# Work moved from VectorE to GpSimd in the attention part of a one-core decoder step

## The reference, cut to what matters

```python
h = rms_norm(x, norm_attn)                       # then one input projection of h
o_sb  = stick_breaking(sb_q, sb_k, sb_v)         # 8 heads x 64, causal
p2    = softmax(q k_sel); o_sel = p2 @ v_sel     # 8 heads, 2 kv groups
pw    = softmax(q k_win); o_win = pw @ v_win
o_nsa = g0 * o_cmp + g1 * o_sel + g2 * o_win     # per-head sigmoid gates
mix   = concat(rms_norm(o_sb, norm_sb_out), rms_norm(o_nsa, norm_nsa_out))
x     = x + mix @ w_out
h2    = rms_norm(x, norm_ffn)                    # rows for the router and the experts
y     = top-1 of 4 groups, top-2 of 4 gated experts on h2
out   = rms_norm(x + y, norm_final)
```

## Time and profile before

| what | value |
|---|---|
| median of three runs | 818.14 us |
| lowest, highest | 817.3, 818.15 us |
| profiled execution: span | 814.9 us |
| between the span and the median run | 3.2 us |
| PE busy | 736.1 us (90%) |
| DVE busy | 381.6 us (47%) |
| ACT busy | 218.5 us (27%) |
| POOL busy | 56.9 us (7%) |

### The profile page before, as it was taken

The page is one execution under the profiler, slowest core; times in us unless marked ns, Lnnn a source line. Parts: engine busy times, 40 slices in busy tenths (PEclk is TensorE's granted clock), DMA queues, the critical chain, the costliest instruction groups (busy, mean ns, idle before and its releaser), DMA issues.

```text
span 814.9 us, 12490 instructions
## 1 busy us (share of the span) xinstructions
PE 736.1 (90%) x4713; PEld 397.4 (49%) x4713; DVE 381.6 (47%) x884; ACT 218.5 (27%) x561; POOL 56.9 (7%) x87
## 2 busy tenths in 40 slices
PE   4986899997999788989979977789999999999987
PEld 2454456444645544545545643355555545454532
DVE  5421103385220667886877845365144332423145
ACT  1211111111221446656756831001110101010113
POOL 0111000120000000000000000210000000000040
PEclk9999899999999579999999998689999999999999
DMA  9136881558334960000000246789899999999992
GB/s 329 33 92 168 236 308 44 199 140 271 115 132 123 288 252 1 1 3 1 1 27 1 104 153 235 223 265 335 284 400 407 402 406 396 408 402 399 408 389 108
DMA packets 99423, 172.98 MB, mean 212 GB/s; under 512 B 21314, under 2 KB 38562, under 8 KB 99330
## 3 DMA queue, kind: packets, MB, share of 16 engines
q1 hardware_dynamic: 87986, 150.76, 52.3%
q10 hardware_dynamic: 8112, 11.24, 3.7%
q0 software_dynamic: 3264, 10.17, 3.5%
HBM read 152.95 MB, written 21.28 MB: 214 GB/s over the span
## 4 chain that ended last, share of the span: by engine, by line
PE 56%; DVE 8%; DMA 5%; ACT 4%; issue 3%; SPq 1%; ACTq 0%; DVEq 0%
PE bank L2392 18%; PE bank L1797 5%; PE bank L2825 5%; PE bank L2383 4%; PE bank L2807 4%; PE bank L2426 4%; PE bank L1724 3%; PE bank L1743 3%; DMA reg<-w_down 2%; PE bank L2516 1%; PE bank L2511 1%; SPq L1965 1%; DMA work<-h_rows,ids 1%; PE bank L1726 1%; PE bank L2375 1%
## 5 line engine op out<-in xcount | busy, mean ns | idle before, releaser
L2825 PE MATMUL bank<-reg 128*128 128x512 f32 (+1 forms) x384 | 165.8, 578 | 1.2 <-DVE reg L2766 0.9
L2392 PE MATMUL bank<-reg,qreg 128*32 128x128 f32 (+2 forms) x848 | 130.4, 389 | 0.8 <-issue 0.8
L2825 PEld LDWEIGHTS bank<-reg 128*128 128x128 f32 x384 | 71.7, 195 | 69.4 <-issue 66.7
L2392 PEld LDWEIGHTS bank<-reg,qreg 128*32 128x32 f32 (+2 forms) x848 | 66.8, 139 | 59.5 <-issue 48.2
L2807 PE MATMUL bank<-cf,reg 128*128 128x128 f32 (+1 forms) x384 | 63.2, 285 | 24.0 <-DVE reg L2757 9.9
L1797 PE MATMUL bank<-reg 128*128 128x512 f32 x128 | 65.9, 640 | 0.4 <-DVE x L1504 0.3
L2807 PEld LDWEIGHTS bank<-cf,reg 128*128 128x128 f32 (+1 forms) x384 | 43.3, 145 | 42.1 <-issue 35.4
L2682 ACT ACTIVATE work<-bank 128x128 f32<-128x128 f32 (+6 forms) x107 | 40.9, 413 | 45.3 <-PE bank L2807 44.7
L2766 DVE COPY work<-bank 128x128 f32<-128x128 f32 (+4 forms) x56 | 23.2, 429 | 51.0 <-PE bank L2807 50.8
L1212 ACT ACTIVATE reg<-bank,st 128x128 f32<-128x128 f32 (+3 forms) x64 | 33.2, 525 | 35.5 <-DVE st L1372 35.4
L1743 PE MATMUL bank<-work,vreg 128*64 128x128 f32 x480 | 39.2, 295 | 2.4 <-DVE work L2766 2.4
(11 more groups left out here) (338 smaller groups left out, 929.4 us busy)
## 6 DMA issues: line engine op xcount, KB each, us to landing
reg<-w_gate SPq DMA_DIRECT2D x12, 2048.0 KB, 20.2
reg<-w_up SPq DMA_DIRECT2D x12, 2048.0 KB, 23.9
reg<-w_down SPq DMA_DIRECT2D x12, 2048.0 KB, 20.8
reg<-w_in SPq DMA_DIRECT2D x16, 512.0 KB, 5.9
expert_rows<-vreg SPq DMA_DIRECT2D x11, 512.0 KB, 5.3
reg<-cache_sb_k SPq DMA_DIRECT2D x16, 256.0 KB, 4.4
reg<-cache_sb_v SPq DMA_DIRECT2D x16, 256.0 KB, 4.6
qreg<-w_up SPq DMA_DIRECT2D x2, 2048.0 KB, 16.6
```

The lines of the kernel that those rows point to most:

```text
L2392: ins = T.matmul(bank[which][rows, at_:at_ + w], rowsT[b][:, k, r0:r0 + n], w_[:, k, h * w:(h + 1) * w], start=(k == 0), stop=(k == KD - 1))
L2825: ins = nc.tensor.matmul(at("m", ("proj", n))[:, 0:w], hT[:, k, i * P:(i + 1) * P], win[:, pos % 2, k, 0:w], start=(k == 0), stop=(k == KD ...
```

## The change

- `share`: DVE only inverts the sums. POOL scales the probabilities, with the inverse and the gate as two per-row factors in one instruction a head (64 instructions of 128 x 128 to 128 x 512).
- `scale_wout`: POOL does it, in eight steps of one block, from agenda place 15 on, every 40 units.
- `mix_sums`: POOL does it, for all five tiles, as two additions of two inputs (512 and then 256 elements a row) in place of one reduction.
- `h2` of the decode tile, tile 0 and tile 1 (`POOL_ROWS`): POOL does it, as a scaling by the row's factor and a product with the gain (1024 elements a row each) in place of one DVE instruction. Tiles 2 and 3 stay on DVE.
- `top`: one maximum instruction over both heads' banks in place of two.
- Some semaphores are merged, and the router's weights get one of their own.

The diff, cut to its core:

```diff
+    POOL_ROWS = tile_order[:3]
...
-    for q, k in enumerate(range(0, KD, 2)):
-        place((60, 130, 230, 330)[q], scale_wout, k)
+    for k in range(KD):
+        place(15 + 40 * k, scale_wout, k)
...
+    def unit_sums(u):
+
+        q = nsa_at[u] % 4
+        return st[:, 2 * q:2 * q + 2]
...
     def gps_more(pool, kind, key):
-        if kind == "slots":
+        G = nc.gpsimd
+        if kind == "share":
+            i, b, p = key
+            n, w = (i + 1) * P, unit_sums(key)
+            gate = gate_rows(i)[:, b, p, :]
+            if key == nsa_units[0]:
+                sg.wait(pool, "gates", 0)
+            sg.wait(pool, "inverse", key)
+            for e in range(2):
+                prob = prob_of(key, e)[:, 0:n]
+                ins = G.tensor_scalar(prob, prob, w[:, e:e + 1], gate[:, e:e + 1], ALU.mult, ALU.mult)
+            ins.then_inc(sg["shared"], 1)
+        elif kind == "scale_wout":
+            k0, = key
+            if k0 == 0:
+                pool.wait_ge(sg["gain_in"], 64)
+            pool.wait_ge(sg["w_out_sb" if k0 < REP else "w_out_nsa"], 16 if k0 < REP else 32)
+            G.tensor_scalar(w_out[:, k0, :], w_out[:, k0, :], gainT[:, k0:k0 + 1], None, ALU.mult
+                            ).then_inc(sg["w_scaled"], 1)
+        elif kind == "mix_sums":
+            i, = key
+            r = ROWS[i]
+            four = squares[:, :, 0:r].rearrange("p (b k) q -> p b k q", b=2)
+            sg.wait(pool, "squares", i)
+            if i != QT:
+                sg.wait(pool, "t_full", ("ssq", tile_order[tile_order.index(i) - 1]))
+            G.tensor_tensor(four[:, :, 0:2], four[:, :, 0:2], four[:, :, 2:4], ALU.add).then_inc(sg["square_sums"], 1)
+            sg.wait(pool, "square_sums", ("half", i))
+            G.tensor_tensor(square_sums[:, :, 0:r], four[:, :, 0], four[:, :, 1], ALU.add).then_inc(sg["square_sums"], 1)
+        elif kind == "h2" and key[0] in POOL_ROWS:
+            i, = key
+            r = ROWS[i]
+            sg.wait(pool, "rstd", ("ffn", i))
+            G.tensor_scalar(h2[0:r], x[0:r, i, :], small[0:r, 12:13], None, ALU.mult).then_inc(sg["h2"], 1)
+            sg.wait(pool, "h2", ("normed", i))
+            G.tensor_tensor(h2[0:r], h2[0:r], gain[0:r, :], ALU.mult).then_inc(sg["h2"], 1)
+        elif kind == "slots":
...
-            for e, ring in enumerate(("ga", "gb")):
-                top = 32 + 2 * (q % 4) + e
-                sg.wait(dve, ring + "_full", key)
-                V.tensor_reduce(st[:, top:top + 1], at(ring, key)[:, 0:n], AX.X, ALU.max, negate=True
-                                ).then_inc(sg["arg"], 1)
+            top = 32 + 2 * (q % 4)
+            sg.wait(dve, "ga_full", key)
+            sg.wait(dve, "gb_full", key)
+            V.tensor_reduce(st[:, top:top + 2], psum[:, 2:4, 0:n], AX.X, ALU.max, negate=True).then_inc(sg["arg"], 1)
         elif kind == "share":
-            i, b, p = key
-            n, q = (i + 1) * P, nsa_at[key]
-            w = st[:, 2 * (q % 4):2 * (q % 4) + 2]
-            gate = gates[:, i, :].rearrange("p (g r t) -> p r t g", g=GROUPS, r=REP)[:, p, b, :]
+            w = unit_sums(key)
             sg.wait(dve, "gb_act", key)
-            link(V.reciprocal(w, w))
-            link(V.tensor_tensor(w, w, gate, ALU.mult))
-            for e in range(2):
-                ins = V.tensor_scalar(prob_of(key, e)[:, 0:n], prob_of(key, e)[:, 0:n], w[:, e:e + 1], None, ALU.mult)
-            ins.then_inc(sg["shared"], 1)
+            V.reciprocal(w, w).then_inc(sg["inverse"], 1)
```

More of the change, by code:

```diff
@@ L462, in norm @@
             step("norm", i)
-            sg.mark(f"x{i}", i, 16)
+            sg.mark(f"tile{i}", i, 16)
             sg.mark("ssq", ("attn", i))
@@ L597, in mix_sums @@
         step("mix_sums", i)
+        sg.mark("square_sums", ("half", i))
         sg.mark("square_sums", i)
@@ L628, in ffn_scale @@
         sg.mark("rstd", ("ffn", i))
+    POOL_ROWS = tile_order[:3]
     def ffn_rows(i):
         step("h2", i)
+        if i in POOL_ROWS:
+            sg.mark("h2", ("normed", i))
         sg.mark("h2", i)
@@ L701, in top @@
         step("top", *u)
-        sg.mark("arg", u, 2)
+        sg.mark("arg", u)
     def exp(u):
@@ L708, in share @@
         step("share", *u)
+        sg.mark("inverse", u)
         sg.mark("shared", u)
@@ L854, in body @@
     route_weights(QT - 1)
-    for name, by in (("const", 16), ("const_b", 16), ("gain_attn", 16), ("table_zero", 16), ("y_zero", 16 * EXTRA + 16), ("router_in", 80),
-                     ("iota", 1), ("zero", 1), ("act_chain", 0), ("dve_chain", 0), ("pe_chain", 0)):
+    for name, by in (("const", 32), ("gain_attn", 16), ("table_zero", 16), ("y_zero", 16 * EXTRA + 16), ("router_in", 80),
+                     ("iota", 1), ("zero", 1), ("act_chain", 0), ("dve_chain", 0), ("pe_chain", 0),
+                     ("router_scaled", 1)):
         sg.mark(name, 0, by)
@@ L998, in load_router @@
     def load_router(sp):
-        sp.dma_start(cb[:, :], a["const_b"]).then_inc(sg["const_b"], 16)
+        sp.wait_ge(sg["const"], 16)
+        sp.dma_start(cb[:, :], a["const_b"]).then_inc(sg["const"], 16)
         sp.wait_ge(sg["zero"], 1)
@@ L1400, in dve_more @@
                 dve.wait_ge(sg["router_in"], 80)
[L1401 to L1406, removed]
+                V.tensor_tensor(wr[:, :, 0:20], wr[:, :, 0:20], gainR[:, :].unsqueeze(2).to_broadcast([P, KD, 20]), ALU.mult
+                                ).then_inc(sg["router_scaled"], 1)
         elif kind == "sample_small":
@@ L1465, in dve_more @@
                             ).then_inc(sg["c_max"], 1)
[L1466 to L1473, removed]
         elif kind == "cmp_norm":
@@ L1515, in dve_more @@
                                    small[0:r, 12:13]).then_inc(sg["ssq"], 1)
-        elif kind == "h2":
+        elif kind == "h2" and key[0] not in POOL_ROWS:
             i, = key
@@ L1706, in pe_more @@
             if key == units[SEL]:
-                pe.wait_ge(sg["const_b"], 16)
+                pe.wait_ge(sg["const"], 32)
                 for j in range(len(proj)):
@@ L1779, in pe_more @@
                 if i == QT:
-                    sg.wait(pe, "w_scaled", 4 * group + 2)
+                    sg.wait(pe, "w_scaled", 4 * group + 3)
                 if i == QT and group == 0:
@@ L1804, in pe_more @@
             acquire(pe, "t", ("parts", i))
+            if i == QT:
+                pe.wait_ge(sg["router_scaled"], 1)
             for half in range(2):
@@ L2355, in expert_dve @@
             if i == 0:
-                dve.wait_ge(sg["gain_final"], 16)
+                sg.wait(dve, "gain_in", "final")
             sg.wait(dve, "ssq_final", i)
@@ L2620, in _ @@
                     src = a["x_prompt"][0, i * P:(i + 1) * P, :] if i < QT else a["x_sample"][:, 0, :]
-                    sp.dma_start(x[0:ROWS[i], i, :], src).then_inc(sg[f"x{i}"], 16)
+                    sp.dma_start(x[0:ROWS[i], i, :], src).then_inc(sg[f"tile{i}"], 16)
                     if i == 0:
@@ L2746, in _ @@
                 r = ROWS[i]
-                dve.wait_ge(sg[f"x{i}"], 16)
+                dve.wait_ge(sg[f"tile{i}"], 16)
                 if i >= 2:
```

4 lines of the change are left out of this document (2 added, 2 removed).

## The result

The changed kernel takes 828.27 us (median of 4 runs, 826.04 to 830.2) against 818.14; the ratio is 1.013 with a 95% interval of 1.0101 to 1.016. It is slower by some 10 us. I had forecast 820.4, with 817.3 to 823.5 as its own range and 811 to 828 around all the rivals: the sign was right, the size was wrong, and so was the make-up of the sum.

What follows compares the result with a forecast made beforehand. PE was taken to set the end, with its attention stalls for DVE and ACT deciding. 5.7 + 0 - 2.9 - 0.8 - 1.3 + 0.4 + 0.6 (longer half clock) + 0.6 = +2.3, so 820.4 us (817.3 to 823.5; all rivals 811 to 828).

Steps and rivals of the forecast that it cites:

- R3: Rival: POOL scaling with two pointer factors costs 2 to 4 ns an element, normed rows end late; 828 us, chance 0.10.
- Normed rows, decode tile and tile 0, +5.7: Attention: POOL's rows delay ACT's DMA by 2.9 us at tile 0 and 2.8 at the decode tile; bounds +3.5 to +20.
- Tile 1, 0: Normed rows of tile 1: POOL is free early enough, so no cost; range -1.1 to +3 us.
- W_out's rows, -2.9: Opening, 300 to 320 us: moving these rows off DVE shortens PE's waits, by 1.3 and 1.6 us.
- clock -0.8: Opening, 316 to 319.4 us: shorter waits keep PE's clock full, saving 1.6 us at one chance in two.
- opening -1.3: Stretch from 264 to 300 us: PE gains a third of the 4.5 us it lacks.
- step 4: Opening: PE's clock staying full, -0.8 us at one chance in two, and a third of 4.5 us from 264 to 300, -1.3.
- Square sums, +0.4: `mix_sums` on POOL takes 2.1 us against 1.92; only the last tile's makes PE wait longer, 0.1 to 1.2 us.
- Shares on POOL, 0: Shares take 1.4 us a unit against 0.98 on DVE, covered by some 5 us before their transposes; no cost.
- Ports, +0.6: POOL and DVE in each other's way where they overlap: +0.6 us in the sum.
- R4: Rival: DVE and POOL take turns at the ports for whole instructions, delaying DVE's two-input scans; 824 us, chance 0.10.
- One maximum, 0: Scores: one maximum for two saves a fixed cost of about 0.1 us, hidden behind PE's second score; 0.

Runs made afterwards that it cites:

- before_sync: The kernel before with the stores of the first two normed tiles issued by SyncE and nothing else: 812.23 us, ratio 0.9948.
- two_factors_sync: The changed kernel with 1.0 as second factor in POOL's scalings and the first two normed tiles' stores issued by SyncE: 807.24 us, ratio 0.9887.
- experiments 2 and 3: The changed kernel with normed rows back on DVE (809.34 us, 0.9936), then with W_out's rows back on DVE too (808.73 us, 0.9888).
- (7): The changed kernel, one-factor scaling kept, with the stores of the three normed tiles issued by SyncE instead of ACT: 813.48 us, ratio 0.9953.
- experiment 9: The changed kernel with shares, W_out's rows and normed rows on DVE: 0.9985; the kernel before with one maximum for two heads and nothing else: 0.9983.
- rows_by_sync: The changed kernel with only the stores of the three normed tiles moved from ACT to SyncE: 813.48 us, ratio 0.9953.
- rows_dve: The changed kernel with all normed rows back on DVE, W_out's rows staying on POOL with one factor: 809.34 us, ratio 0.9936.
- (10): The changed kernel with 1.0 as second factor and SyncE's stores for two normed tiles: 807.24 us; the kernel before with those stores only: 812.23 us.

## Why the prediction was wrong

The step that failed is the price of a scaling on POOL, 1.2 us for 1024 elements "since one operand is a tensor in both". It was read from the copy and applied to two forms. For the shares, which have two factors, it holds (0.82 against 0.68). For the eleven instructions with one factor it is 2.85 (W_out's rows, mean) and 2.83 to 3.75 (normed rows). R3 had the right fear but for the wrong form: it priced scaling "with two pointer factors" at 2 to 4 ns, and gave 828 us for it, at a chance of 0.10. Mending the form takes 8 of the 10 us away and gives 820.8, my forecast to half a microsecond, but that is partly luck, since other terms were off and cancelled. Term by term:

1. *Normed rows, decode tile and tile 0, +5.7.* By the ruler, these two pairs are 5.0 and 5.8 us longer than before (9.60 to 14.60 and 10.82 to 16.58). Of the excess over 5.7, 3.3 us are the scaling's price (twice 1.65); the other 1.8 go with a lower granted clock behind the longer stalls, 0.79 from 360 to 380 and 0.75 from 420 to 440 (rows below), where the kernel before had 0.92 from 340 to 360 and 0.91 from 400 to 420. The pairs between, 18th to 25th, took 48.05 us in place of 46.10, but that is not shown to be the clock's: in before_sync and two_factors_sync, with shorter stalls, they took 48.03 and 48.04. And the proper base was not the kernel before. Kept on DVE, the rows would have come sooner than before. Seen so, the move costs 16 to 17 us (experiments 2 and 3), of which 14 hang on ACT's queue (7). The changed kernel's stretches behind the two stalls, PE busy and clock as in the windows above:

```profile
360.00:380.00 20.00, 17.20 (x91) 8.88 (x92) 7.90 (x23) 12.35 (x30) 5.29 (x7) 0.79 0.02 3
...
420.00:440.00 20.00, 14.31 (x81) 8.04 (x83) 12.21 (x25) 11.25 (x24) 6.57 (x7) 0.75 0.08 28
```

2. *Tile 1, 0.* The store there goes 14.4 us later than before, and at tile 0 it goes 12.3 us later. Of the 2 us between, 1.4 lie from the 32nd inverse to the store (6.59 to 7.95), in the range, and 0.6 elsewhere.
3. *W_out's rows, -2.9, clock -0.8, opening -1.3.* The 300 to 320 stretch did gain 2.6 us and its clock stayed up, as step 4 had it one time in two. The 264 to 300 stretch lost 4.2 us where I had +1.3, because eight instructions of 2.85 us stand between the shares. "100 units of agenda time or more" was true for W_out's rows themselves, and said nothing about the shares queued behind them. In the sum the opening was worth 0.8 us (ruler 79.3 to 78.5), not 5.0. With 1.1 us each it would have been worth 3.9 to 8.1: the ruler is 71.2 to 75.4 us in the four kernels with that form. (The third of 4.5 us in step 4 is 1.5 and not 1.3, so my own sum would have been +2.1.)
4. *Square sums, +0.4.* PE waits 1.9 us for the last tile's; before it was 1.7. That is the 0.2 by which 2.1 exceeds 1.92, and not 0.4.
5. *Shares on POOL, 0.* They were hidden where they ran, as I said. But what they freed was worth 8 us (experiment 9), at least in front of the normed rows. I had written that between these places less of DVE's load buys nothing, and overlooked that at the normed rows the shares stood in front of the rows in DVE's queue.
6. *Ports, +0.6; R4 at 3 to 4 us.* DVE does stand behind POOL's instructions, as R4 said, and at tile 0 and the decode tile that makes PE stand 6.1 us once ACT is out of the way (7). But not every overlap costs it the whole rest: in the changed kernel one scan of the opening took 1.62 us in place of 0.42 and one at tile 1 took 2.07 in place of 1.20, while the other scans took at most 0.35 more than alone. Two comparisons would size its part together with the longer way of the rows: 0.0017 or 1.4 us with one factor (rows_by_sync over rows_dve, whose store still waits in ACT's queue) and 0.0046 or 3.8 us with two (10). Neither is clear of its intervals, so R4's 3 to 4 us are neither shown nor ruled out; what decided lay elsewhere.
7. *One maximum, 0.* Not told from zero (9).

Together: the shares, sums and maximum -9, W_out's rows about +4 in their form, the normed rows +16 to 17: +11 to 12 by parts, +10.6 measured. The +4 for W_out's rows is the weakest of these, as its intervals overlap. What stays open is how much of the normed rows' cost is the clock and how much the waits, of PE for ACT and for DVE; they came together here. Nor was it tried why the form with one factor is slow.

## What to carry to other kernels

Price an operation on another engine by its exact form, not by its number of tensor inputs: on this chip's GpSimd a scaling by one factor took 2.85 us for 1024 elements and the same with a second factor of 1.0 took 1.1. When a step is moved off an engine, compare with what that engine would then do, not with what it did: the 8 us that one move gained (the shares) were spent, and more, by another (the normed rows). And before lengthening a step, look at who waits for it in order: a store in ACT's queue turned 3.6 to 6 us of GpSimd work into a standstill of copies and exponentials, and from an idle engine's queue the same work cost little.

## What the runs showed of the hardware

- One-factor TENSOR_SCALAR on GpSimd: 914 ns for 256 elements, 1548 for 512, 2854 (mean of 8) for 1024, and 2844 and 3748 for the normed rows of two tiles; it takes as long on 8 rows as on 128 (2.83 us). With two factors: 450 for 128, 760 to 824 for 512, 1102 to 1189 for 1024. A product of 1024 elements with a broadcast factor: 1894; with two whole tensors: 2338; a copy: 1037.
- At the decode tile and at tile 0 a DVE TENSOR_SCALAR of 8 elements from SBUF to SBUF, started inside POOL's scaling, and a DVE product with two SBUF inputs, started inside POOL's product, ended with POOL's instruction to within 0.04 us; a reduction was not delayed.
- Started 0.53 to 0.91 us into a one-factor scaling of 1024 elements, DVE's two-input instructions L1508 and L1409 took 0.05 to 0.45 us more than alone and ended some 1.45 us before POOL did; a scan started 1.3 us in was not delayed (0.39 us).
- In the changed kernel the granted clock is 0.79 from 360 to 380 us and 0.75 from 420 to 440, right behind PE's stalls of 6.51 and 7.40 us; in rows_dve, where no such stall is over 2.3, no stretch of 20 us from 320 to 480 is below 0.91.
